# Chunk attention: dividing by the row sums after the values' product in place of before it

## The chip, the cores and the metric

The kernel runs on one core of one Trainium2 chip. The metric is the device time of one execution in microseconds (us); the median of three runs of the kernel before is 1773.39 us (1770.58 to 1775.37).

## What is computed

The program is a two-layer encoder for 512 tokens of width 1024, all in 32-bit floats. The second layer begins with chunked softmax attention: 16 heads of 64 columns, chunks of 64 tokens that see themselves and all earlier ones here, with a learned bias by distance. Cut to what matters:

```python
s = jnp.einsum('bqhd,bkhd->bhqk', q_c, k_c) * scale + bias
s = jnp.where((band_pos + start) >= 0, s, -1e30)
p = jax.nn.softmax(s, axis=-1)
return jnp.einsum('bhqk,bkhd->bqhd', p, v_c)
# all chunks: o, then o @ w_out
```

## The kernel before

The engines are programmed by hand: each has its own instruction list in a fixed order, and they meet only at semaphores. TensorE (PE) multiplies, VectorE (DVE) and ScalarE (ACT) work on its results in PSUM (8 banks of 128x512), GpSimd (POOL) masks the bias, and SyncE issues DMAs.

Chunk attention works through 8 pairs of heads, m = 0 to 7; e = 0, 1 is the head in the pair, i = 0 to 3 a block of 128 queries, which needs keys 0 to (i+1)*128, so blocks have 128 to 512 columns. For a pair:

- `ca_scores_pe` multiplies queries with keys in the order i = 3, 2, 0, 1, both heads side by side on 64 rows of the array each; the last, i = 1, waits for the first two sums of the same pair, which free its bank. `sums` on VectorE adds the bias, takes the maximum of each row (`c_s2`, L2039) and negates it (`c_max`, L2043).
- `exp` on ScalarE (L2011) makes the unnormalized probabilities and their row sums; `rescale` on VectorE (L2053, L2057) takes the reciprocals and multiplies the probabilities in place.
- `ca_turn_p_pe` transposes them (L1959) in eight groups n = 0 to 7 (s = n // 2 is the block of keys, e = n % 2), through a ring of three PSUM banks, 4 to 6. `ca_copy` takes each group to SBUF: n = 0, 2, 5, 7 on ScalarE (L1985), n = 1, 3, 4, 6 on VectorE (L1987), by the list `COPY`. A group can be written once the copy three groups earlier is done.
- `ca_values_pe` (L1969) multiplies values with these, both heads side by side on 64 columns of the array each, into bank 7. ScalarE rounds the result to `c_oT[0]` (out_hi here, L2028), and VectorE keeps the rest in `c_oT[1]` (`out_lo`, L2047). The output projection "co" multiplies with both and waits for the last `out_lo`.

The pairs are staggered by the order in each list. In round m TensorE does turns(m), scores(m+2), values(m). ScalarE waits for the maxima of m+1 and then does the eight exps of m+1 with its four copies of m between them, and at the end of the round waits for values(m) and does out_hi(m). VectorE does out_lo(m-1), its copies of m with the rescale of (m+1, e=0) before the last, sums(m+2), and the rescale of (m+1, e=1).

Of the kernel before, what the change touches and what calls it, by code (L numbers as in the profile page):

```python
# [7 lines left out]
F32 = mybir.dt.float32  # L8
F32R = mybir.dt.float32r
ALU = mybir.AluOpType  # L10
ACT = mybir.ActivationFunctionType
AX = mybir.AxisListType.X

P = 128
D = 1024
SEQ = 512
# [3 lines left out]
TT = SEQ // P  # L20
# [17 lines left out]
CH = 16  # L38
CD = D // CH
# [8 lines left out]
LEVELS = 5  # L48
# [27 lines left out]
def build_program(nc, A):  # L76
    ctx = ExitStack()
    with ctx:
        def tensor_at(name, at, dtype, *shape):

            assert at % 8 == 0
            with nc.sbuf_tensor(f"below_{name}", [P, at], F32), nc.sbuf_tensor(name, [P, *shape], dtype) as v:
                return v[(slice(None),) * (1 + len(shape))]

        def rounded(name, at, *shape):
            return tensor_at(name, at, F32R, *shape)

        with nc.sbuf_tensor("params", [P, N_PAR], F32) as par:
# [4 lines left out]
        ps = ctx.enter_context(nc.psum_tensor("ps", [P, 8, 512], F32))  # L93
# [15 lines left out]
                   "glu_landed": ("wab_in", 16), "g_v": ("u_s", 8),  # L109
                   "cat_hi": ("go_sq", TT), "cat_lo": ("go_n", TT), "mem_kept": ("cat_s5", 1),  # L110
                   "f_gate": ("sv_y", LEVELS * TT), "f_rmm": ("r_kw", 2 * NCH), "f_rbc": ("r_om", NCH), "eps_rows": ("sv_d", LEVELS * TT),
                   "c_pv2": ("sv_u", LEVELS * TT),
                   "c_mask": ("sv_mask", LEVELS * TT), "c_rec": ("sv_yc", LEVELS * TT),
                   "s5_gate": ("s5_fn", 4), "g_roots": ("s5_den", 1), "g_coef": ("s5_arg", 1), "logit_rows": ("s5_dt", 1), "logit_turned": ("s5_rd", 1),
                   "s5_pad": ("conv", 12), "y_v": ("conv", 20), "y_a": ("u_s", 4)}
# [24 lines left out]
        def sem(name):  # L140
            name = named(name)[0]
            if name not in sems:
                sems[name] = ctx.enter_context(nc.semaphore(name))
            return sems[name]
# [55 lines left out]
        ident = ccol("ident")  # L200
# [142 lines left out]
        def after(name, n):  # L343

            return n + named(name)[1]
# [1082 lines left out]
        at_b, at_c, at_d, at_e, at_f = (arena + 4096 * n for n in range(1, 6))  # L1428
# [416 lines left out]
        c_max, c_neg, c_sum, c_rec = cs(2, 2, TT), cs(2, 2, TT), cs(2, 2, TT), cs(2, 2, TT)  # L1845
        ck_rows = rows(high_b)
        cqT, ckT = feat(high_c), feat(high_d)
        CA_ROWS, CA_EXP = (3, 2, 0, 1), (3, 2, 1, 0)
        CA_TRI = P * TT * (TT + 1) // 2

        def p_c(m, e, i):
            at = base + (2 * (m % 2) + e) * CA_TRI + P * (i * (i + 1) // 2)
            return reg(at, (i + 1) * P)

        def pT_c(e, s):
            at = base + (4 + e) * CA_TRI + P * (s * TT - s * (s - 1) // 2)
            return reg(at, (TT - s) * P)
# [3 lines left out]
            return ps[:, bank + e, c0:c0 + (i + 1) * P]  # L1861

        c_oT = (rounded("c_o_hi", arena, KT, SEQ), rounded("c_o_lo", at_b, KT, SEQ))


        def ca_proj_pe(pe):
# [83 lines left out]
        def ca_turn_p_pe(pe, m):  # L1950
            for n in range(8):
                s, e = n // 2, n % 2
                g = 8 * m + n
                if g >= 3:
                    pe.wait_ge(sem(COPY[(g - 3) % 8][0]), 4 * ((g - 3) // 8) + COPY[(g - 3) % 8][1])
                for i in range(s, TT):
                    if s == 0:
                        pe.wait_ge(sem(RESCALE[i][0]), after(RESCALE[i][0], RESCALE[i][1] * (2 * m + e) + RESCALE[i][2]))
                    ins = pe.transpose(ps[:, 4 + g % 3, i * P:(i + 1) * P], p_c(m, e, i)[:, s * P:(s + 1) * P], ident)  # L1959
                ins.then_inc(sem("c_tr"), 1)  # L1960

        def ca_values_pe(pe, m):
            if m > 0:
                pe.wait_ge(sem("c_ol"), m)
            for s in range(TT):
                for e in range(2):
                    pe.wait_ge(sem(COPY[2 * s + e][0]), 4 * m + COPY[2 * s + e][1])
                    h = 2 * m + e
                    ins = pe.matmul(ps[64 * e:64 * e + 64, 7, s * P:SEQ], v_rows[:, s, h * CD:(h + 1) * CD], pT_c(e, s),  # L1969
                                    start=(s == 0), stop=(s == TT - 1), skip_group_check=True)  # L1970
            ins.then_inc(sem("c_o"), 1)


        COPY = [("c_pa", 1), ("c_pv", 1), ("c_pa", 2), ("c_pv", 2), ("c_pv", 3), ("c_pa", 3), ("c_pv", 4), ("c_pa", 4)]
        RESCALE = [("c_pv2", 4, 4), ("c_pv2", 4, 3), ("c_pv2", 4, 2), ("c_pv2", 4, 1)]

        def ca_copy(eng, m, n):
            s, e = n // 2, n % 2
            g = 8 * m + n
            eng.wait_ge(sem("c_tr"), g + 1)  # L1980
            if m >= 1:
                eng.wait_ge(sem("c_o"), m)
            dst, src = pT_c(e, s), ps[:, 4 + g % 3, s * P:SEQ]
            if COPY[n][0] == "c_pa":
                eng.activation(dst, src, ACT.Copy).then_inc(sem("c_pa"), 1)  # L1985
            else:
                eng.tensor_copy(dst, src).then_inc(sem("c_pv"), 1)  # L1987
# [20 lines left out]
        def ca_act(a):  # L2008
            def exp(m, e, i):
                p = p_c(m, e, i)  # L2010
                a.activation(p, p, ACT.Exp, bias=c_neg[:, m % 2, e, i:i + 1], accum_out=c_sum[:, m % 2, e, i:i + 1]).then_inc(sem("c_exp"), 1)  # L2011

            a.wait_ge(sem("c_max"), 1)
            for e in range(2):
                for i in CA_EXP:
                    exp(0, e, i)
            for m in range(CH // 2):
                if m + 1 < CH // 2:
                    a.wait_ge(sem("c_max"), m + 2)
                for e in range(2):  # L2020
                    for j in range(4):
                        if m + 1 < CH // 2:
                            exp(m + 1, e, CA_EXP[j])
                        n = 4 * e + j
                        if COPY[n][0] == "c_pa":
                            ca_copy(a, m, n)
                a.wait_ge(sem("c_o"), m + 1)
                a.activation(c_oT[0][:, m, :].rearrange("p (i n) -> p i n", i=TT),  # L2028
                                  ps[:, 7, :].rearrange("p (i n) -> p i n", i=TT)[:, :, ::-1], ACT.Copy).then_inc(sem("c_oc"), 1)

        def ca_dve(v):
            def sums(m):
                v.wait_ge(sem("c_mask"), after("c_mask", 2 * m + 2))
                if m >= 2:
                    v.wait_ge(sem("c_tr"), 8 * (m - 1))
                for n, i in enumerate(CA_ROWS):
                    v.wait_ge(sem("c_s"), 4 * m + (1, 3, 3, 4)[n])
                    for e in range(2):
                        v.tensor_tensor_reduce(out=p_c(m, e, i), in0=ca_score(i, e),  # L2039
                                                    in1=bias_ring[:, (2 * m + e) % 4, BAND_W - (i + 1) * P:BAND_W], scale=1.0, scalar=-3.0e38,  # L2040
                                                    op0=ALU.add, op1=ALU.max, accum_out=c_max[:, m % 2, e, i:i + 1]).then_inc(sem("c_s2"), 1)
                v.wait_ge(sem("c_s2"), 8 * m + 8)
                v.tensor_scalar(c_neg[:, m % 2], c_max[:, m % 2], -1.0, None, ALU.mult).then_inc(sem("c_max"), 1)  # L2043

            def out_lo(m):
                v.wait_ge(sem("c_oc"), m + 1)
                v.tensor_tensor(c_oT[1][:, m, :].rearrange("p (i n) -> p i n", i=TT),  # L2047
                                ps[:, 7, :].rearrange("p (i n) -> p i n", i=TT)[:, :, ::-1],
                                c_oT[0][:, m, :].bitcast(F32).rearrange("p (i n) -> p i n", i=TT), ALU.subtract).then_inc(sem("c_ol"), 1)

            def rescale(m, e):
                v.wait_ge(sem("c_exp"), 8 * m + 4 * e + 4)
                v.reciprocal(c_rec[:, m % 2, e], c_sum[:, m % 2, e]).then_inc(sem("c_rec"), 1)  # L2053
                v.wait_ge(sem("c_rec"), after("c_rec", 2 * m + e + 1))
                for i in (3, 2, 1, 0):
                    p = p_c(m, e, i)
                    v.tensor_scalar(p, p, c_rec[:, m % 2, e, i:i + 1], None, ALU.mult).then_inc(sem("c_pv2"), 1)  # L2057

            sums(0)
            sums(1)  # L2060
            rescale(0, 0)
            rescale(0, 1)
            for m in range(CH // 2):
                if m > 0:
                    out_lo(m - 1)
                for n in range(8):
                    if COPY[n][0] == "c_pv":
                        ca_copy(v, m, n)
                    if n == 4 and m + 1 < CH // 2:
                        rescale(m + 1, 0)  # L2070
                if m + 2 < CH // 2:
                    sums(m + 2)
                if m + 1 < CH // 2:
                    rescale(m + 1, 1)
            out_lo(CH // 2 - 1)

        def ca_pool(g):
# [371 lines left out]
```

## Time and profile before

| | before |
|---|---|
| median of three runs | 1773.39 us |
| the profiled execution, own time | 1774.5 us |
| its span on the core | 1772.7 us |
| mean granted TensorE clock | 0.982 |
| busy in the span: TensorE, VectorE, ScalarE | 94%, 44%, 34% |
| chunk attention's rounds | about 1084 to 1171 us of the span |

One execution was traced. A row of one line of the code has the least, median and longest duration in ns and the first and last start in us. A row of the timeline is: start in us from the span's start, duration in us, engine, line, operation, output and input, shape, count; in brackets the idle time of the engine before it and what ended it. PEclk is the clock that TensorE was granted as a share of 2.4 GHz. A 32-bit product is two records of TensorE, a transpose is one. An engine may start its next instruction some 0.1 us before the one before has ended, so what an instruction occupies is read from start to start.

### The profile page before, as it was taken

Reading aid. Unit: us, or ns where it says so; the run is one execution under the profiler, and the core shown is the slowest. Engines: PE = TensorE matmul, PEld = TensorE weight load, DVE = VectorE, ACT = ScalarE, POOL = GpSimd, SP = SyncE. Lnnn points to the kernel's source line nnn. Section 1 sums busy time; section 2 is a strip of 40 time slices with the busy share of each in tenths; the row PEclk is TensorE's granted clock in tenths of the full one; section 3 lists DMA queues with packets and bytes.
Section 4 is the critical chain, followed back from the end, with each engine's and each line's share of the span. In section 5 each row is a group of like instructions: output and inputs, shape, how many; then the busy total and the mean of one; then the engine's idle time right before and its main releaser. Section 6 shows DMA issues by size and latency. Waiting matters only on the chain.

```text
span 1772.7 us, 22589 instructions
## 1 busy us (share of the span) xinstructions
PE 1659.4 (94%) x9358; PEld 1354.6 (76%) x9358; DVE 786.1 (44%) x1023; ACT 611.5 (34%) x991; POOL 230.0 (13%) x305
## 2 busy tenths in 40 slices
PE   6998589999989999999999998899998999999999
PEld 5887568777858888888888885468776878888887
DVE  5752834545353444443225436844444444444222
ACT  5224143345342432222114335634353332332110
POOL 2681223310000111111000000000000011111000
PEclk9996899999999999999999998999999999999999
DMA  6306001125202233332222330304410333333221
GB/s 206 96 24 119 1 5 58 63 95 189 72 24 69 74 97 101 101 104 95 95 95 88 102 119 24 96 24 137 147 50 24 96 95 95 95 95 95 95 95 71
DMA packets 146801, 151.85 MB, mean 86 GB/s; under 512 B 8864, under 2 KB 109344, under 8 KB 146592
## 3 DMA queue, kind: packets, MB, share of 16 engines
q1 hardware_dynamic: 146720, 150.69, 27.8%
q8 instruction: 60, 0.98, 0.2%
q14 instruction: 21, 0.17, 0.0%
HBM read 147.53 MB, written 3.15 MB: 85 GB/s over the span
## 4 chain that ended last, share of the span: by engine, by line
PE 86%; DVE 8%; ACT 3%; issue 2%; DMA 0%; SPq 0%; POOL 0%; DVEq 0%; ACTq 0%
PE ps L325 24%; PE ps L327 24%; PE ps L326 23%; PE ps L1612 2%; PE ps L1635 2%; PE ps L1969 1%; PE ps L955 1%; DVE sb L2039 1%; PE ps L1070 1%; ACT w_hi L293 1%; PE ps L1229 1%; PE ps L417 1%; ACT sb L2011 1%; PE ps L1240 1%; DVE sb L2057 1%
## 5 line engine op out<-in xcount | busy, mean ns | idle before, releaser
L325 PE MATMUL ps<-h_hi,w_hi 128*128 128x512 f32 x864 | 336.9, 390 | 4.0 <-DVE w_lo L1783 3.9
L326 PE MATMUL ps<-h_lo,w_hi 128*128 128x512 f32 x864 | 336.1, 389 | 0.0
L297 DVE TENSOR_TENSOR w_lo<-raw,w_hi 128x2048 fp32r<-128x2048 f32 x70 | 160.4, 2292 | 395.4 <-ACT w_hi L293 395.4
L293 ACT ACTIVATE w_hi<-raw 128x2048 fp32r<-128x2048 f32 x84 | 160.7, 1915 | 421.2 <-PE ps L327 420.6
L327 PE MATMUL ps<-h_hi,w_lo 128*128 128x512 f32 x704 | 273.9, 389 | 0.0
L325 PEld LDWEIGHTS ps<-h_hi,w_hi 128*128 128x128 f32 x864 | 162.2, 188 | 38.5 <-issue 4.7
L326 PEld LDWEIGHTS ps<-h_lo,w_hi 128*128 128x128 f32 x864 | 162.2, 188 | 33.7
L1783 DVE TENSOR_TENSOR w_lo<-raw,w_hi 128x2048 fp32r<-128x2048 f32 x44 | 138.1, 3138 | 53.5 <-ACT w_hi L1765 53.5
L327 PEld LDWEIGHTS ps<-h_hi,w_lo 128*128 128x128 f32 x704 | 132.1, 188 | 27.5
L1765 ACT ACTIVATE w_hi<-raw 128x2048 fp32r<-128x2048 f32 x44 | 84.3, 1916 | 160.9 <-PE ps L327 160.9
L325 PE MATMUL ps<-w_hi,a_hi 128*128 128x512 f32 x352 | 137.3, 390 | 1.7 <-DVE up L1781 1.7
L326 PE MATMUL ps<-w_lo,a_hi 128*128 128x512 f32 x352 | 137.0, 389 | 0.0
L327 PE MATMUL ps<-w_hi,a_lo 128*128 128x512 f32 x352 | 136.9, 389 | 0.0
L1793 POOL CAST a_hi<-up 128x512 f32 x44 | 27.0, 613 | 843.0 <-DVE up L1781 843.0
L325 PE MATMUL ps<-w_hi,h_hi 128*128 128x512 f32 x320 | 124.7, 390 | 2.3 <-DVE h_lo L430 2.3
L327 PE MATMUL ps<-w_hi,h_lo 128*128 128x512 f32 x320 | 124.5, 389 | 0.0
L326 PE MATMUL ps<-w_lo,h_hi 128*128 128x512 f32 x320 | 124.5, 389 | 0.0
L1781 DVE TENSOR_TENSOR up<-up,ps 128x512 f32<-128x512 f32 x44 | 30.3, 688 | 192.4 <-PE ps L327 188.6
L1761 ACT ACTIVATE up<-up 128x512 f32<-128x512 f32 x44 | 27.8, 632 | 152.0 <-DVE up L1777 152.0
L325 PEld LDWEIGHTS ps<-w_hi,a_hi 128*128 128x128 f32 x352 | 66.1, 188 | 16.0 <-DVE up L1781 2.5
L327 PEld LDWEIGHTS ps<-w_hi,a_lo 128*128 128x128 f32 x352 | 66.1, 188 | 13.9
L326 PEld LDWEIGHTS ps<-w_lo,a_hi 128*128 128x128 f32 x352 | 66.1, 188 | 13.7
(369 smaller groups left out, 2686.1 us busy)
## 6 DMA issues: line engine op xcount, KB each, us to landing
raw<-in_f_w_gate SPq DMA_DIRECT2D x44, 512.0 KB, 4.0
raw<-in_f_w_up SPq DMA_DIRECT2D x44, 512.0 KB, 5.2
raw<-in_f_w_down SPq DMA_DIRECT2D x44, 512.0 KB, 4.1
raw<-in_xa_w_kv SPq DMA_DIRECT2D x16, 1024.0 KB, 5.0
raw<-in_c_w_qkv SPq DMA_DIRECT2D x12, 1024.0 KB, 5.0
raw<-in_ab_w_in SPq DMA_DIRECT2D x10, 1024.0 KB, 5.3
raw<-in_xa_w_q SPq DMA_DIRECT2D x8, 1024.0 KB, 5.1
raw<-in_xa_w_out SPq DMA_DIRECT2D x8, 1024.0 KB, 5.0
```

The costliest lines, as they stand in the source:

```text
L293: a.activation(w_hi[:, n % 2, :], raw[n % 2], ACT.Copy).then_inc(sem("w_hi"), 1)
L297: v.tensor_tensor(w_lo(n)[:, n % 2, :], raw[n % 2], w_hi[:, n % 2, :].bitcast(F32), ALU.subtract).then_inc(sem("w_lo"), 1)
L325: pe.matmul(out, a[0], b[0], start=start, stop=False)
L326: pe.matmul(out, a[0], b[1], start=False, stop=False)
L327: return pe.matmul(out, a[1], b[0], start=False, stop=stop)
L1612: ins = pe.matmul(ps[:, 2 * (h % 2) + i // 2, (i % 2) * 256:(i % 2) * 256 + 256], qT[:, 2 * h + d, i * P:(i + 1) * P], xk_T[:, 2 * h + d, ...
L1635: ins = pe.matmul(ps[:, 6 + d, :], xv[:, s, h * XD + d * P:h * XD + (d + 1) * P], pT_x[h % 2][:, s, :], start=(s == 0), stop=(s == 1))
L1761: a.activation(gsil[:, s, :], gsil[:, s, :], ACT.Silu).then_inc(sem(f"f{l}_silu"), 1)
L1765: a.activation(w_hi[:, slot, :], raw[slot], ACT.Copy).then_inc(sem("w_hi"), 1)
L1781: v.tensor_tensor(prod[:, s, :], gsil[:, s, :], ps[:, 2 * s + 1, :], ALU.mult).then_inc(sem(f"f{l}_free"), 1)
L1783: v.tensor_tensor(w_lo(n0)[:, slot, :], raw[slot], w_hi[:, slot, :].bitcast(F32), ALU.subtract).then_inc(sem("w_lo"), 1)
L1793: g.tensor_copy(aT[0][:, at], prod[:, s, :]).then_inc(sem(f"f{l}_ahi"), 1)
```

## The change

The probabilities are no longer multiplied. `rescale` is gone; one reciprocal of a 128x8 block for each pair (`reciprocals`) takes its place. After its eight groups of transposes TensorE has a ninth: eight products of a 128x64 broadcast of the reciprocals with the identity, both heads side by side on 64 columns of the array each, into bank 6, once the copy of group 5 is done. They spread the reciprocals over a block laid out as the output is. ScalarE copies that block to SBUF (`c_rbc`, two buffers) at the end of its round. VectorE multiplies the values' output in bank 7 with it into the same buffer (`out_scaled`), ScalarE rounds from there (`out_hi`), now in the next round between its second and third exp, and VectorE's `out_lo` follows after copy 3. The transposes wait for the exps alone, and values(m) waits for `out_scaled(m-1)` where it waited for `out_lo(m-1)`. The ring of three banks is counted anew in each round (n % 3), with the ninth group in it.

```diff
         def ca_turn_p_pe(pe, m):
             for n in range(8):
                 s, e = n // 2, n % 2
-                g = 8 * m + n
-                if g >= 3:
-                    pe.wait_ge(sem(COPY[(g - 3) % 8][0]), 4 * ((g - 3) // 8) + COPY[(g - 3) % 8][1])
+                bank_copied(pe, m, n)
                 for i in range(s, TT):
                     if s == 0:
-                        pe.wait_ge(sem(RESCALE[i][0]), after(RESCALE[i][0], RESCALE[i][1] * (2 * m + e) + RESCALE[i][2]))
-                    ins = pe.transpose(ps[:, 4 + g % 3, i * P:(i + 1) * P], p_c(m, e, i)[:, s * P:(s + 1) * P], ident)
+                        pe.wait_ge(sem("c_exp"), 8 * m + 4 * e + CA_EXP.index(i) + 1)
+                    ins = pe.transpose(ps[:, 4 + n % 3, i * P:(i + 1) * P], p_c(m, e, i)[:, s * P:(s + 1) * P], ident)
                 ins.then_inc(sem("c_tr"), 1)
+            bank_copied(pe, m, 8)
+            pe.wait_ge(sem("c_rec"), after("c_rec", m + 1))
+            for i in range(TT):
+                for e in range(2):
+                    ins = pe.matmul(ps[64 * e:64 * e + 64, 6, i * P:(i + 1) * P], c_rec[:, m % 2, e, i:i + 1].broadcast_to([P, CD]), ident,
+                                    start=True, stop=True)
+            ins.then_inc(sem("c_tr"), 1)
 
         def ca_values_pe(pe, m):
             if m > 0:
-                pe.wait_ge(sem("c_ol"), m)
+                pe.wait_ge(sem("c_om"), after("c_om", m))
...
+        def bank_copied(pe, m, n):
+            m, n = (m, n - 3) if n >= 3 else (m - 1, n + 6)
+            if m >= 0 and n < 8:
+                pe.wait_ge(sem(COPY[n][0]), 4 * m + COPY[n][1])
+            elif m >= 0:
+                pe.wait_ge(sem("c_rb"), after("c_rb", m + 1))
...
+            def out_hi(m):
+                a.wait_ge(sem("c_om"), after("c_om", m + 1))
+                a.activation(c_oT[0][:, m, :], c_rbc(m), ACT.Copy).then_inc(sem("c_oc"), 1)
...
-                a.wait_ge(sem("c_o"), m + 1)
-                a.activation(c_oT[0][:, m, :].rearrange("p (i n) -> p i n", i=TT),
-                                  ps[:, 7, :].rearrange("p (i n) -> p i n", i=TT)[:, :, ::-1], ACT.Copy).then_inc(sem("c_oc"), 1)
+                        if n == 1 and m > 0:
+                            out_hi(m - 1)
+                a.wait_ge(sem("c_tr"), 9 * m + 9)
+                if m >= 2:
+                    a.wait_ge(sem("c_ol"), m - 1)
+                a.activation(tiles(c_rbc(m)), tiles(ps[:, 6, :])[:, :, ::-1], ACT.Copy).then_inc(sem("c_rb"), 1)
+            out_hi(CH // 2 - 1)
...
+            def out_scaled(m):
+                v.wait_ge(sem("c_o"), m + 1)
+                v.wait_ge(sem("c_rb"), after("c_rb", m + 1))
+                v.tensor_tensor(tiles(c_rbc(m)), tiles(ps[:, 7, :])[:, :, ::-1], tiles(c_rbc(m)), ALU.mult).then_inc(sem("c_om"), 1)
...
-            def rescale(m, e):
-                v.wait_ge(sem("c_exp"), 8 * m + 4 * e + 4)
-                v.reciprocal(c_rec[:, m % 2, e], c_sum[:, m % 2, e]).then_inc(sem("c_rec"), 1)
-                v.wait_ge(sem("c_rec"), after("c_rec", 2 * m + e + 1))
-                for i in (3, 2, 1, 0):
-                    p = p_c(m, e, i)
-                    v.tensor_scalar(p, p, c_rec[:, m % 2, e, i:i + 1], None, ALU.mult).then_inc(sem("c_pv2"), 1)
+            def reciprocals(m):
+                v.wait_ge(sem("c_exp"), 8 * m + 8)
+                v.reciprocal(c_rec[:, m % 2], c_sum[:, m % 2]).then_inc(sem("c_rec"), 1)
...
             sums(0)
             sums(1)
-            rescale(0, 0)
-            rescale(0, 1)
+            reciprocals(0)
             for m in range(CH // 2):
                 if m > 0:
-                    out_lo(m - 1)
+                    out_scaled(m - 1)
                 for n in range(8):
                     if COPY[n][0] == "c_pv":
                         ca_copy(v, m, n)
-                    if n == 4 and m + 1 < CH // 2:
-                        rescale(m + 1, 0)
+                    if n == 3 and m > 0:
+                        out_lo(m - 1)
                 if m + 2 < CH // 2:
                     sums(m + 2)
                 if m + 1 < CH // 2:
-                    rescale(m + 1, 1)
+                    reciprocals(m + 1)
+            out_scaled(CH // 2 - 1)
             out_lo(CH // 2 - 1)
```

## Rows read from the trace of the kernel before

**Rows 1.** The page: the chain that ended last, by engine.
```profile
PE 86%; DVE 8%; ACT 3%; issue 2%; DMA 0%; SPq 0%; POOL 0%; DVEq 0%; ACTq 0%
```
**Rows 2.** Windows: length; busy (count) of PE, PEld, DVE, ACT, POOL; PEclk; DMA.
```profile
1123.89:1133.57 9.68, 7.90 (x56) 4.55 (x54) 8.74 (x34) 6.24 (x22) 0.29 (x2) 1.00 0.21 56
```
**Rows 3.** Timeline, one round, from scores(4) to the next sums.
```profile
1122.51 2.00 PE L1947 MATMUL ps<-sb 64*128 64x512 f32 x12
...
1123.89 0.69 DVE L2039 CUSTOM_DVE_ANT_0 sb<-ps,sb 128x512 f32<-128x512 f32 x1
...
1125.25 0.70 PE L1947 MATMUL ps<-sb 64*128 64x256 f32 x4 [0.74 <-DVE sb L2039]
...
1125.88 2.37 PE L1969 MATMUL ps<-sb 128*64 128x512 f32 x16
...
1127.30 0.17 DVE L2043 TENSOR_SCALAR sb<-sb 128x8 f32<-128x8 f32 x1
...
1128.19 0.66 PE L1959 MATMUL ps<-sb 128*128 128x128 f32 x4
1128.30 0.60 ACT L2028 ACTIVATE c_o_hi<-ps 128x512 fp32r<-128x512 f32 x1 [3.44 <-PE ps L1969]
1128.80 0.71 ACT L2011 ACTIVATE sb<-sb 128x512 f32<-128x512 f32 x1
...
1133.57 0.69 DVE L2039 CUSTOM_DVE_ANT_0 sb<-ps,sb 128x512 f32<-128x512 f32 x1
```
**Rows 4.** Timeline, one round: a rescale, ScalarE's copies 0 and 5.
```profile
1119.83 0.58 ACT L1985 ACTIVATE sb<-ps 128x512 f32<-128x512 f32 x1
...
1122.50 1.28 DVE L2057 TENSOR_SCALAR sb<-sb 128x512 f32<-128x512 f32 x4
...
1123.45 0.37 ACT L1985 ACTIVATE sb<-ps 128x256 f32<-128x256 f32 x1
```
**Rows 5.** By form, 1084:1176, VectorE: xcount | busy, mean ns | idle before.
```profile
L1987 DVE COPY sb<-ps 128x512 f32<-128x512 f32 x8 | 5.5, 691 | 1.7 <-PE ps L1959 1.4
...
L2047 DVE TENSOR_TENSOR c_o_lo<-ps,c_o_hi 128x512 fp32r<-128x512 f32 x8 | 5.5, 690 | 3.5 <-ACT c_o_hi L2028 3.1
...
L2053 DVE RECIPROCAL sb<-sb 128x4 f32<-128x4 f32 x16 | 2.8, 175 | 2.8 <-ACT sb L2011 2.8
```
**Rows 6.** Timeline, ScalarE from SBUF to SBUF, 128x512, and the next.
```profile
598.12 0.63 ACT L1761 ACTIVATE up<-up 128x512 f32<-128x512 f32 x1
598.66 1.90 ACT L1765 ACTIVATE w_hi<-raw 128x2048 fp32r<-128x2048 f32 x1
```
**Rows 7.** TensorE, timeline and line: broadcast by identity; pairs on 64 columns.
```profile
595.12 1.05 PE L1743 MATMUL ps<-sb 128*128 128x128 f32 x8
595.93 0.48 PE L325 MATMUL ps<-h_hi,w_hi 128*128 128x512 f32 x1
...
L844 PE MATMUL ps<-sb x128: 222/222/271, 174.4 to 178.1; 128*64 128x64 f32 x128
```
**Rows 8.** Timeline: scores(1), sums(1), first exp of pair 1, sums(2), sums(7).
```profile
1090.65 4.62 PE L1947 MATMUL ps<-sb 64*128 64x512 f32 x16 [0.88 <-DVE sb L2039]
...
1092.88 0.69 DVE L2039 CUSTOM_DVE_ANT_0 sb<-ps,sb 128x512 f32<-128x512 f32 x1 [2.08 <-PE ps L1947]
...
1096.88 0.72 ACT L2011 ACTIVATE sb<-sb 128x512 f32<-128x512 f32 x1 [1.58 <-DVE sb L2043]
...
1104.53 0.69 DVE L2039 CUSTOM_DVE_ANT_0 sb<-ps,sb 128x512 f32<-128x512 f32 x1
...
1152.91 0.68 DVE L2039 CUSTOM_DVE_ANT_0 sb<-ps,sb 128x512 f32<-128x512 f32 x1
```
**Rows 9.** Timeline, the end of the stage.
```profile
1171.49 0.50 PE L325 MATMUL ps<-w_hi,c_o_hi 128*128 128x512 f32 x1 [1.42 <-DVE c_o_lo L2047]
```
**Rows 10.** Timeline and window (as rows 2): the stage's start, after a wait.
```profile
1088.54 1.22 PE L1947 MATMUL ps<-sb 64*128 64x256 f32 x4 [2.76 <-DVE sb L2039]
...
1089.00:1091.00 2.00, 1.12 (x6) 0.40 (x6) 1.76 (x11) 0.17 (x1) 0.00 (x0) 0.50 0.00 0
```

More of the change, by code:

```diff
@@ L111, in build_program @@
                    "f_gate": ("sv_y", LEVELS * TT), "f_rmm": ("r_kw", 2 * NCH), "f_rbc": ("r_om", NCH), "eps_rows": ("sv_d", LEVELS * TT),
-                   "c_pv2": ("sv_u", LEVELS * TT),
+                   "c_rb": ("sv_u", LEVELS * TT), "c_om": ("sv_t", (LEVELS - 1) * TT),
                    "c_mask": ("sv_mask", LEVELS * TT), "c_rec": ("sv_yc", LEVELS * TT),
@@ L1863, in build_program, with c_rbc, tiles @@
         c_oT = (rounded("c_o_hi", arena, KT, SEQ), rounded("c_o_lo", at_b, KT, SEQ))
+        c_rbc2 = tensor_at("c_rbc", at_f + 2056, F32, 2, SEQ)
+        def c_rbc(m):
+            return c_rbc2[:, m % 2, :]
+        def tiles(o):
+            return o.rearrange("p (i n) -> p i n", i=TT)
         def ca_proj_pe(pe):
@@ L1974, in build_program @@
         COPY = [("c_pa", 1), ("c_pv", 1), ("c_pa", 2), ("c_pv", 2), ("c_pv", 3), ("c_pa", 3), ("c_pv", 4), ("c_pa", 4)]
-        RESCALE = [("c_pv2", 4, 4), ("c_pv2", 4, 3), ("c_pv2", 4, 2), ("c_pv2", 4, 1)]
+        def bank_copied(pe, m, n):
[4 more added lines that the diff above has]
+                pe.wait_ge(sem("c_rb"), after("c_rb", m + 1))
         def ca_copy(eng, m, n):
             s, e = n // 2, n % 2
-            g = 8 * m + n
-            eng.wait_ge(sem("c_tr"), g + 1)
+            eng.wait_ge(sem("c_tr"), 9 * m + n + 1)
             if m >= 1:
                 eng.wait_ge(sem("c_o"), m)
-            dst, src = pT_c(e, s), ps[:, 4 + g % 3, s * P:SEQ]
+            dst, src = pT_c(e, s), ps[:, 4 + n % 3, s * P:SEQ]
             if COPY[n][0] == "c_pa":
@@ L2034, in sums @@
                 if m >= 2:
-                    v.wait_ge(sem("c_tr"), 8 * (m - 1))
+                    v.wait_ge(sem("c_tr"), 9 * (m - 1))
                 for n, i in enumerate(CA_ROWS):
@@ L2043, in sums @@
                 v.tensor_scalar(c_neg[:, m % 2], c_max[:, m % 2], -1.0, None, ALU.mult).then_inc(sem("c_max"), 1)
+            def out_scaled(m):
+                v.wait_ge(sem("c_o"), m + 1)
+                v.wait_ge(sem("c_rb"), after("c_rb", m + 1))
+                v.tensor_tensor(tiles(c_rbc(m)), tiles(ps[:, 7, :])[:, :, ::-1], tiles(c_rbc(m)), ALU.mult).then_inc(sem("c_om"), 1)
             def out_lo(m):
                 v.wait_ge(sem("c_oc"), m + 1)
-                v.tensor_tensor(c_oT[1][:, m, :].rearrange("p (i n) -> p i n", i=TT),
-                                ps[:, 7, :].rearrange("p (i n) -> p i n", i=TT)[:, :, ::-1],
-                                c_oT[0][:, m, :].bitcast(F32).rearrange("p (i n) -> p i n", i=TT), ALU.subtract).then_inc(sem("c_ol"), 1)
-            def rescale(m, e):
-                v.wait_ge(sem("c_exp"), 8 * m + 4 * e + 4)
-                v.reciprocal(c_rec[:, m % 2, e], c_sum[:, m % 2, e]).then_inc(sem("c_rec"), 1)
-                v.wait_ge(sem("c_rec"), after("c_rec", 2 * m + e + 1))
-                for i in (3, 2, 1, 0):
-                    p = p_c(m, e, i)
-                    v.tensor_scalar(p, p, c_rec[:, m % 2, e, i:i + 1], None, ALU.mult).then_inc(sem("c_pv2"), 1)
+                v.tensor_tensor(c_oT[1][:, m, :], c_rbc(m), c_oT[0][:, m, :].bitcast(F32), ALU.subtract).then_inc(sem("c_ol"), 1)
+            def reciprocals(m):
+                v.wait_ge(sem("c_exp"), 8 * m + 8)
+                v.reciprocal(c_rec[:, m % 2], c_sum[:, m % 2]).then_inc(sem("c_rec"), 1)
             sums(0)
             sums(1)
-            rescale(0, 0)
-            rescale(0, 1)
+            reciprocals(0)
             for m in range(CH // 2):
                 if m > 0:
-                    out_lo(m - 1)
+                    out_scaled(m - 1)
                 for n in range(8):
```

## The prediction, made before the changed kernel was run

> **What bounds the kernel now.** I read the page's chain first: TensorE carries 86% of what ended last [rows 1]. Over the whole kernel, then, work taken from VectorE is worth nothing; it can only count where TensorE waits for it. The window of one attention round shows such a place: of 9.68 us VectorE is busy 8.74, TensorE 7.90, ScalarE 6.24 [rows 2]. So the first impression is that VectorE sets the round here, and the change takes work from it. But busy time alone doesn't say what the round will be afterwards; for that one has to follow the order of the lists. The timeline of one round gives this order and its delays [rows 3]. I call T the start of a round's sums (1123.89 us). From there: the second sum lets TensorE do the last scores at T+1.36, values follow at T+1.99, the maxima are negated at T+3.41 and known at T+3.58, and the next round's transposes start at T+4.30 and end at T+4.96. The next sums start at T+9.68. ScalarE waits 3.44 us for values(m) before its out_hi, so it has room.
>
> **What VectorE loses and gains.** Per pair it loses two rescales, 2 x 1.28 us [rows 4], and one of two reciprocals of 0.18 [rows 5]. It gains out_scaled, which the trace doesn't have; the nearest row is out_lo, a product of the same shape from PSUM, 0.69 [rows 5]. In all about 2.0 us less in each round. That would be a gain if VectorE's list ran without new gaps. It won't.
>
> **The new order on ScalarE and TensorE.** The ninth group goes into bank 6 and waits for the copy of group 5. That is ScalarE's third copy, and its list puts six of the next pair's exps, two other copies and now out_hi(m-1) ahead of it. TensorE's list is in order: scores(m+2) stand behind the ninth group, and VectorE's next sums wait for scores(m+2). Before, the last transposes waited only for VectorE's copies, and scores started at 1122.51, while copy 5 started only at 1123.45 [rows 3, 4]. So a loop closes: sums, maxima, ScalarE's exps and copies, ninth group, scores, sums. I walk it with T as above:
> - The exp of (m+2, e=0, i=3) can start at T+3.6 and is done before the transposes are; so copy 0 starts when group 0 has been transposed, T+4.96+0.03 = T+4.99.
> - From copy 0 to copy 5 ScalarE's list took 1123.45 - 1119.83 = 3.62 us without a gap [rows 4]. Out_hi now stands in it. Its operation is not in the trace; another activation of 128x512 from SBUF to SBUF takes 0.63 and lets the next start after 598.66 - 598.12 = 0.54 [rows 6]. Copy 5 takes 0.37 [rows 4]. It ends at T + 4.99 + 3.62 + 0.54 + 0.37 = T+9.52, and TensorE starts the ninth group at T+9.57.
> - The ninth group has no row. Four products of a 128x128 broadcast with the identity occupy TensorE for 595.93 - 595.12 = 0.81 us [rows 7]; here there are eight of half the width. If the two heads run side by side the time is that, about 0.85; if not, double, 1.7. Pairs on 64 columns elsewhere: 128 records of 64 columns in 3.7 us; 16 records of 128 columns are a quarter of that work, 0.94 [rows 7]. I take 0.95, as this row is the nearest, and keep 0.8 and 1.7 as the ends.
> - Scores start at T+10.52. Their first pair of products took 2.23 from start to the first sum at half clock, 1090.65 to 1092.88 [rows 8]; at full clock 1.12 and a hop of 0.04. The next sums start at T+11.68.
>
> The round becomes 11.68 us where it was 9.68: 2.0 us longer. VectorE lies beside it with slack: its out_scaled, three of its copies and out_lo are done some 2 us before copy 5, and it then idles until the new sums. So the 2.0 us saved on VectorE turn into waiting, ScalarE's copy of the reciprocals' block (0.60, like the old out_hi from PSUM [rows 3]) runs while TensorE does scores and costs nothing, and the round is longer by what TensorE now waits for ScalarE.
>
> **The first round and the end.** In round 0 no rescale delays the transposes and there is no out_hi. ScalarE starts pair 1's exps at 1096.88 [rows 8]; copy 5 starts 0.71 [rows 3] + 3.62 = 4.33 us later, at 1101.2, and ends at 1101.6. Ninth group and scores, 0.05+0.95+1.16, put sums(2) at 1103.75, where they were at 1104.53 [rows 8]: 0.8 us gained at full clock. At half clock the last two terms double, and 1.3 are lost; I take the gain, since the wait before it gets shorter. From sums(2) to sums(7) are 5 rounds, 1104.53 to 1152.91 [rows 8]: 5 x 2.0 = 10.0 us lost.
> From sums(7) to the first product of "co" were 1171.49 - 1152.91 = 18.58 us [rows 8, 9]. Now, with T at sums(7): the ninth group of pair 6 at T+9.57, no scores, values(6) from T+10.52 to T+12.75 (2.23 to occupy; from 1125.88 to the next group at 1128.19 it is 2.31 with a hop [rows 3]). Pair 7 has no rescale and no exps beside it, but its copies pass through the ring: VectorE starts out_scaled(6) when values(6) end, T+13.0, and is done with it at T+13.7; copy 1 ends at T+14.6 (0.69 [rows 5], behind its group's transposes), copy 3 at T+15.2, out_lo(6) at T+15.8, copy 4 at T+16.2 (the narrower copies at less in proportion); group 7 waits for it, the ninth group runs T+16.35 to T+17.30, values(7) until T+19.68. Then, one after the other, out_scaled 0.69, out_hi 0.63 and out_lo 0.69 with hops of 0.05, 2.2 in all. Co starts at T+21.9: 3.3 us lost.
> Sum: -0.8 + 10.0 + 3.3 = 12.5 us. The profiled execution took 1774.5 us, so 1787.0; against the median of 1773.4 the same sum gives 1786. The output projection's weights come ahead of their use in either case, and everything behind simply shifts.
>
> **A rule beside a row.** The last pair of scores occupies TensorE for 1125.88 - 1125.25 = 0.63 us until values start [rows 3], though 256 columns at the values' rate (1280 columns in 2.31 us) would be 0.46: a change of the array's shape seems to cost up to 0.17. The Trainium skill (TensorEngine Tiling (Array Packing), Key Properties) says that changing the tiling mode drains the TensorE. The ninth group stands between full-width transposes and scores on 64 rows, so it adds one such change. By the rule I would add 0.17 for each of its places on the loop, seven: 1787; without it 1786, which I keep.
>
> **The rivals.**
> - *It pays, VectorE was the bound.* If copy 5 did not hold TensorE, the round would be what TensorE itself needs: its 7.90 us [rows 2] with the ninth group less overlap, 8.0 to 8.85. Then 5 rounds gain 0.8 to 1.7 each, the first gains up to 2.9 (two rescales and reciprocals, [rows 4, 5]) and the end loses 0.8: 1763 to 1770. It decides for this if the ninth group starts before T+7.5, 2 us earlier than the loop gives it; ScalarE would have to run four of its exps less ahead of copy 5. Nothing in the rows speaks for it. 8 in 100.
> - *It evens out.* Some step on the loop is shorter and the round stays near 9.7: 1769 to 1778. 5 in 100.
> - *The loop, with the heads of the ninth group one after the other.* 0.75 us more in seven places, 5 in all: 1791. The row of pairs on 64 columns speaks against it. 8 in 100.
> - *The granted clock falls.* TensorE now waits about 1.5 us in a stretch for copy 5, besides 0.7 for the sums. After a wait of 2.76 us at the start of the stage the clock read 0.50, that is 1.2 GHz [rows 10]; with waits up to 0.74 it reads 1.00 [rows 2, 3]. In between there is no row. At half clock the parts of TensorE on the loop (scores and values 2.9, group 0 0.4, the ninth group 0.95, first scores 1.1) double, 5.4 us a round; if that holds for half of the rounds, 13 more: 1799, for all, 1813. 9 in 100.
> - *The loop as worked out,* 1781 to 1791: 70 in 100.
>
> **How the numbers follow.** The likeliest gives 1786. The lower end takes a ninth group of 0.8, an out_hi that costs less, a start that gains more and the spread of the runs (1770.6 to 1775.4): 1780. The upper end takes the ninth group at 1.7 or a few rounds at the lower clock: 1796. A measurement tells some 0.3% from no change, 5.3 us: slower is the loop in its three forms, 0.87; same 0.05; faster 0.08.
>
> **What would show it.** In the trace of the changed kernel: rounds of about 11.7 us between first sums; TensorE idle 1.2 to 1.8 us before the ninth group, released by ScalarE's copy; the ninth group 0.85 to 1.1 us; VectorE idle about 3 us before the sums, released by the scores; co starting near 1184. The prediction is wrong if the ninth group doesn't wait for ScalarE, or if the round is under 10.5 us.

## The result, and the profile after

The changed kernel takes 1797.4 us (median of 4 runs) against 1772.0: 1.0142 times the time of before, with a 95% interval of 1.0125 to 1.0159. It is slower, as forecast, but by 25 us where 12.5 were forecast, and 1797.4 lies just outside the range of 1780 to 1796. The profiled execution took 1797.5 us in all, its span 1795.8; it is 23.0 us longer than the profiled execution of the kernel before.

First the timeline of one round of the changed kernel, in the same columns as [rows 3]:

```profile
1117.02 0.69 DVE L2065 CUSTOM_DVE_ANT_0 sb<-ps,sb 128x512 f32<-128x512 f32 x1 [4.51 <-PE ps L1955]
...
1118.39 0.30 PEld L1955 LDWEIGHTS ps<-sb 64*128 64x128 f32 x4 [0.33 <-DVE sb L2065]
...
1121.33 2.32 PE L1965 MATMUL ps<-sb 128*128 128x128 f32 x16
...
1122.02 0.60 ACT L2003 ACTIVATE sb<-ps 128x512 f32<-128x512 f32 x1 [0.52 <-PE ps L1965]
...
1123.12 0.62 ACT L2033 ACTIVATE c_o_hi<-c_rbc 128x512 fp32r<-128x512 f32 x1
...
1124.65 0.65 PE L1965 MATMUL ps<-sb 128*128 128x128 f32 x4 [1.01 <-ACT sb L2003]
...
1126.18 0.37 ACT L2003 ACTIVATE sb<-ps 128x256 f32<-128x256 f32 x1
...
1126.61 1.09 PE L1971 MATMUL ps<-sb 128*64 128x128 f32 x16 [1.30 <-ACT sb L2003]
...
1127.63 2.00 PE L1955 MATMUL ps<-sb 64*128 64x512 f32 x12
...
1128.94 0.69 DVE L2065 CUSTOM_DVE_ANT_0 sb<-ps,sb 128x512 f32<-128x512 f32 x1 [3.42 <-PE ps L1955]
```

The loop of the prediction is there, place by place. With T = 1117.02: copy 0 at T+5.00 (worked out: 4.99), copy 5 at T+9.16 (9.15), the ninth group (L1971) at T+9.59 (9.57), released by ScalarE's copy after TensorE had waited 1.30 us. VectorE waits 3.42 us for the scores (L1955). This round took 11.92 us. The next one starts alike and then goes another way. The same lines, from the ninth group on:

```profile
1138.11 0.36 ACT L2003 ACTIVATE sb<-ps 128x256 f32<-128x256 f32 x1
...
1138.52 1.98 PE L1971 MATMUL ps<-sb 128*64 128x128 f32 x16 [1.29 <-ACT sb L2003]
...
1140.43 2.60 PE L1955 MATMUL ps<-sb 64*128 64x512 f32 x12
...
1142.36 0.69 DVE L2065 CUSTOM_DVE_ANT_0 sb<-ps,sb 128x512 f32<-128x512 f32 x1 [4.91 <-PE ps L1955]
```

ScalarE's copy 5 and the ninth group start where they should, T+9.17 and T+9.58 with T = 1128.94, but the ninth group occupies TensorE for 1.91 us and not 1.02, and the round becomes 13.42. The windows of these microseconds (length, TensorE busy, PEclk, DMA) say why:

```profile
1135.12:1136.57 1.45, 0.44 (x3) 1.00 0.21 81
1137.23:1138.52 1.29, 0.00 (x0) 0.91 0.00 0
1138.52:1139.50 0.98, 0.98 (x10) 0.50 0.00 0
1139.50:1140.40 0.90, 0.90 (x10) 0.50 0.00 0
1140.40:1141.40 1.00, 1.00 (x4) 0.50 0.00 0
1141.40:1142.40 1.00, 1.00 (x8) 0.85 0.00 0
1142.40:1143.70 1.30, 0.63 (x8) 1.00 0.00 0
```

The granted clock is 1.00 while TensorE waits for copy 2 and falls during its wait for copy 5, to 0.50, 1.2 GHz; there it stays through the ninth group and half of the scores. In the other long rounds it falls at the start of the ninth group or inside it, at about 1114.4, 1152.0 and 1165.6 us. By round, from first sum to first sum:

```profile
1104.01:1117.02 13.01, 10.25 (x70) 0.89 0.14 41
1117.02:1128.94 11.92, 9.47 (x72) 0.97 0.18 46
1128.94:1142.36 13.42, 10.43 (x72) 0.87 0.13 39
1142.36:1155.89 13.53, 10.54 (x72) 0.87 0.62 195
```

The fifth takes 13.55. The 0.97 of the round of 11.92 is the rest of the low stretch before it: the clock reads 0.50 in its first 0.8 us and 1.00 from there on. [Rows 2] had 9.68 us at 1.00. The start of the stage has waits and a low clock as in [rows 10]. The clock is back at 1.00 from 1094 us and falls again in the first ninth group, at about 1100.7:

```profile
1100.26 1.55 PE L1971 MATMUL ps<-sb 128*64 128x128 f32 x16 [1.30 <-ACT sb L2003]
1101.74 3.17 PE L1955 MATMUL ps<-sb 64*128 64x512 f32 x12
```

Sums(2) and sums(7) begin at 1104.01 and 1169.44 us, where [rows 8] had 1104.53 and 1152.91. At the end of the stage, in place of [rows 9]:

```profile
1179.02 1.80 PE L1971 MATMUL ps<-sb 128*64 128x128 f32 x16 [1.30 <-ACT sb L2003]
1180.61 3.35 PE L1982 MATMUL ps<-sb 128*64 128x512 f32 x16
1183.89 2.87 PE L1965 MATMUL ps<-sb 128*128 128x128 f32 x19
...
1187.62 1.09 PE L1971 MATMUL ps<-sb 128*64 128x128 f32 x16
1188.55 2.32 PE L1982 MATMUL ps<-sb 128*64 128x512 f32 x16
1193.05 0.79 PE L325 MATMUL ps<-w_hi,c_o_hi 128*128 128x512 f32 x1 [2.18 <-DVE c_o_lo L2078]
```

The ninth group and the values of pair 6 run at the lower clock here too (values 3.28 us from start to start where 2.31 are usual [rows 3]), and so do the first products of co.

### The profile page after: what moved, and what is told of

Read it like the earlier page. It is cut to its first block, busy times and chain, and to the rows that moved or that the text cites. A ratio compares the mean times of both kernels' runs of the same rounds, so it can differ in the third digit from the quotient of the medians.

```text
span 1795.8 us, 22811 instructions
## 1 busy us (share of the span) xinstructions
PE 1676.7 (93%) x9486; PEld 1366.5 (76%) x9486; DVE 770.6 (43%) x959; ACT 616.9 (34%) x999; POOL 230.0 (13%) x305
## 4 chain that ended last, share of the span: by engine, by line
PE 86%; DVE 8%; ACT 4%; issue 2%; DMA 0%; SPq 0%; POOL 0%; DVEq 0%; ACTq 0%
PE ps L325 23%; PE ps L327 23%; PE ps L326 23%; PE ps L1612 2%; PE ps L1635 2%; PE ps L1982 1%; PE ps L1955 1%; ACT sb L2029 1%; PE ps L955 1%; DVE sb L2065 1%; PE ps L1971 1%; ACT w_hi L293 1%; PE ps L1229 1%; PE ps L417 1%; PE ps L1240 1%
```

## The experiments

Each time is told by its ratio to the kernel before on the same chip, with its 95% interval. For the stage itself I give three times from the trace: from the first sum of pair 0 to that of pair 2, the five rounds from there to pair 7, and from there to co's first product. The code ahead of the stage is the same in all, yet the first sum falls anywhere between 1082.9 and 1090.8 us of the span, so the stage is measured from its own start.

| kernel | to pair 2 | five rounds | end | stage against before | ratio |
|---|---|---|---|---|---|
| before | 17.35 | 48.38 | 18.58 | | |
| changed | 18.21 | 65.43 | 23.61 | +22.9 | 1.0142 |
| e1_warm | 16.79 | 59.60 | 22.78 | +14.9 | 1.0068 |
| e2_gap | 14.41 | 48.98 | 23.61 | +2.7 | 0.9993 |
| e3_hi_late | 18.29 | 61.23 | 21.40 | +16.6 | 1.0092 |
| e4_copy5 | 17.14 | 54.60 | 20.99 | +8.4 | 1.0039 |
| e5_ninth1 | 17.19 | 59.17 | 22.90 | +15.0 | 1.0078 |
| e6_no_rescale | 14.40 | 48.09 | 18.24 | -3.6 | 0.9980 |
| e7_gap_order | 14.41 | 46.38 | 20.15 | -3.4 | 0.9986 |
| e8_gap_order2 | 13.90 | 44.88 | 19.51 | -6.0 | 0.9967 |

A ratio of 0.001 is 1.8 us. Between the stage's difference and that of the whole lie up to 4 us (e2), which no run explains. Both ends of the span scatter: the time ahead of the stage by up to 8 us, as said, and the time from co's first product to the end of the span between 599.6 and 602.8 us.

### e1_warm: more work for TensorE in its two waits

```diff
+        def keep_busy(pe, m):
+            pe.wait_ge(sem("c_s2"), 8 * min(m + 2, CH // 2))
+            pe.matmul(ps[:, 0, :], ident, con[:, 0:SEQ], start=True, stop=True)
...
+                if n == 5:
+                    keep_busy(pe, m)
                 bank_copied(pe, m, n)
...
+            keep_busy(pe, m)
             bank_copied(pe, m, 8)
```

> The changed kernel plus 16 products of 512 columns whose result nobody reads (0.85 us each at full clock), two a round, placed where TensorE waits for ScalarE's copies 2 and 5. Theory of loop and clock: the round is set by the loop sums, exps, copy 5, ninth group, scores, and on top of it the waits let the granted clock fall, which costs 1.1 to 1.6 us in four of five rounds and more at the end. Then TensorE kept busy stays at clock 1.00, every round is 11.9 us (after: 13.0, 11.9, 13.4, 13.5, 13.6), the first product of co starts near 1186 us instead of 1193, and the time is 6 to 9 us below the changed kernel: 1.009 to 1.011 of before, although there is more work. Rival, TensorE's added work is what costs (0.9 us of ninth group a round) and the clock is only a companion: 13.6 us more work gives 1.015 to 1.022.

Measured 1.0068 (1.0051 to 1.0085), below the expected 1.009. All five rounds take 11.92 us. The timeline of a round, with the added products at L1960:

```profile
1129.93 1.02 PE L1960 MATMUL ps<-sb 128*128 128x512 f32 x2
...
1131.11 0.66 PE L1971 MATMUL ps<-sb 128*128 128x128 f32 x4
...
1131.60 1.02 PE L1960 MATMUL ps<-sb 128*128 128x512 f32 x2
...
1133.06 1.09 PE L1978 MATMUL ps<-sb 128*64 128x128 f32 x16 [0.44 <-ACT sb L2010]
```

and its window (length; busy of PE, PEld, DVE, ACT, POOL; PEclk; DMA):

```profile
1123.48:1135.39 11.91, 10.64 (x76) 5.93 (x74) 6.86 (x24) 6.98 (x22) 0.29 (x2) 1.00 0.14 44
```

The idle time before the ninth group shrinks from 1.30 us to 0.44, the one before the transposes that wait for copy 2 from 1.01 to almost nothing; the rest of the round stays in its place and the clock reads 1.00. TensorE has 16 more products to do, of 1.02 us each in the timeline, and the kernel is about 13 us faster than the changed one (1.0142 - 1.0068). The traces hold 11.0 of these: 8.1 in the stage, and 3.0 because the first sum came that much earlier, which the added products can't have caused. So the time that a round took over 11.92 came from the granted clock, and the rival in which TensorE's load costs has fallen. The run filled both waits and doesn't tell them apart.

At the end of the stage the added products stand in the way themselves. In the last pair the transposes start at 1171.99 us and the ninth group at 1176.59, 4.60 us later, where the changed kernel needed 3.73 (1183.89 to 1187.62):

```profile
1171.99 2.31 PE L1971 MATMUL ps<-sb 128*128 128x128 f32 x16
1176.59 1.09 PE L1978 MATMUL ps<-sb 128*64 128x128 f32 x16
```

That is 0.9 us which e1 pays and the changed kernel doesn't.

### e2_gap: the ninth group where TensorE waits anyway

```diff
+        def ca_ninth_pe(pe, m):   # the lines of the ninth group, moved here
...
                 if n == 3:
+                    if m >= 2:
+                        ca_ninth_pe(pe, m - 2)
                     pe.wait_ge(sem("c_s2"), 8 * m + 2)
...
-                    v.wait_ge(sem("c_tr"), 9 * (m - 1))
+                    v.wait_ge(sem("c_tr"), 9 * (m - 1) - 1)
```

> The ninth group of round m moves from behind the transposes into scores(m+2), ahead of their last pair of products, where TensorE waits 0.7 us for two sums anyway; for the last two pairs it stays. All other work is the same. Theory of the loop: copy 5 no longer stands between the transposes and the sums, the round falls to 9.3 to 9.8 us, the clock stays at 1.00, co starts at 1170 to 1174 us, and the time is that of the kernel before, 0.998 to 1.002. Rival, the work of the ninth group and out_scaled costs wherever it is put: rounds stay at 10.5 us or more, 1.005 or above.

The sums now wait for the eight groups of transposes only, since the ninth stands behind them. Measured 0.9993 (0.9983 to 1.0002): no difference from the kernel before, and 26 us less than the changed kernel with the same work. Rounds take 9.79 or 9.80 us at clock 1.00. Timeline:

```profile
1118.24 1.09 PE L1949 MATMUL ps<-sb 128*64 128x128 f32 x16
...
1119.27 0.70 PE L1966 MATMUL ps<-sb 64*128 64x256 f32 x4
...
1125.53 0.66 PE L1976 MATMUL ps<-sb 128*128 128x128 f32 x4 [1.01 <-ACT sb L2009]
...
1126.11 2.00 PE L1966 MATMUL ps<-sb 64*128 64x512 f32 x12
...
1127.42 0.69 DVE L2071 CUSTOM_DVE_ANT_0 sb<-ps,sb 128x512 f32<-128x512 f32 x1 [1.02 <-PE ps L1966]
```

The ninth group (L1949) takes its 1.03 us beside the sums, of which TensorE would have waited 0.7, and the scores follow the transposes without a wait for copy 5. What is left is the wait of 1.01 us for copy 2. The end is as long as in the changed kernel, since the last two pairs keep the old order. What cost the 2 us a round was the place of the ninth group in TensorE's list. In the stage e2 is 2.7 us longer than the kernel before: 5.0 at the end and 0.6 in the five rounds, less 2.9 ahead of pair 2.

### e3_hi_late: out_hi behind copy 7

```diff
-                        if n == 1 and m > 0:
-                            out_hi(m - 1)
+                if m > 0:
+                    out_hi(m - 1)
                 a.wait_ge(sem("c_tr"), 9 * m + 9)
...
-                    if n == 3 and m > 0:
-                        out_lo(m - 1)
+                    if n == 3 and m > 1:
+                        out_lo(m - 2)
```

> The changed kernel with out_hi(m-1) at the end of ScalarE's round m, behind copy 7, in place of between its second and third exp; out_lo goes one round later. Same work. Theory of the loop: copy 5 ends 0.52 us earlier, a round at full clock takes 11.4 us and not 11.9, 3 us less over the stage before any effect on the clock: 1.009 to 1.013. Rival, ScalarE's order doesn't set the round: 1.014 as before and rounds of 11.9.

Measured 1.0092 (1.0076 to 1.0109). Rounds of 11.39, 13.02, 12.65, 11.39 and 12.78 us: those without a fallen clock are 0.53 below 11.92, which is what out_hi occupied on the loop. Where the clock falls is now another set of rounds.

### e4_copy5: copy 5 to VectorE, copy 6 to ScalarE

```diff
-        COPY = [("c_pa", 1), ("c_pv", 1), ("c_pa", 2), ("c_pv", 2), ("c_pv", 3), ("c_pa", 3), ("c_pv", 4), ("c_pa", 4)]
+        COPY = [("c_pa", 1), ("c_pv", 1), ("c_pa", 2), ("c_pv", 2), ("c_pv", 3), ("c_pv", 4), ("c_pa", 3), ("c_pa", 4)]
```

> The changed kernel with copy 5 on VectorE and copy 6 on ScalarE. Theory of the loop: the ninth group no longer waits for ScalarE's two exps of the second head, only for copy 2 and VectorE; it starts about 1.0 us earlier, rounds of 10.9 us at full clock and one long wait of TensorE in a round instead of two, so the clock falls less: 1.004 to 1.010. Rival, the round is set by TensorE's work: unchanged, 1.014.

Measured 1.0039 (1.0025 to 1.0053). All five rounds take 10.92 us, 1.00 us less than at full clock before. Windows of two of them:

```profile
1101.57:1112.49 10.92, 8.93 (x72) 1.00 0.16 49
1112.49:1123.41 10.92, 8.93 (x72) 1.00 0.17 50
```

The wait for copy 2 is still 1.0 us in each round, and the clock stays at 1.00: with this one wait, the 0.7 us for the sums and 0.3 us ahead of the ninth group it doesn't fall in these rounds, with 1.3 us in place of the 0.3 it does.

### e5_ninth1: two of the ninth group's eight products

```diff
-            for i in range(TT):
+            for i in range(1):
                 for e in range(2):
                     ins = pe.matmul(ps[64 * e:64 * e + 64, 6, i * P:(i + 1) * P], ...
```

> The changed kernel with two of the ninth group's eight products, those of the first block of queries; for the other blocks the outputs are divided by what bank 6 held. All waits stay. Theory of the loop: what the products occupy, 1.02 us at full clock, shrinks to about 0.25, so a round at full clock takes 11.15 us where it took 11.92; the waits for copies 2 and 5 stay and the clock still falls in some rounds: 1.008 to 1.011. Rival, the wait for copy 5 alone is what costs: rounds of 11.9, 1.013 or more.

Measured 1.0078 (1.0060 to 1.0097), a little below what was expected. Rounds of 11.26, 12.08, 11.28, 11.56 and 12.99 us: the two shortest have the lower clock only in their first 0.9 and 1.4 us, beside the sums, and are 0.66 below 11.92, 0.1 less of a saving than worked out. The six products are worth 0.66 us a round. The rest of the 2.1 us that e2 took off a round lies in the wait ahead of the ninth group and in its other two products.

### e6_no_rescale: the kernel before without the rescale

```diff
-                        pe.wait_ge(sem(RESCALE[i][0]), after(RESCALE[i][0], RESCALE[i][1] * (2 * m + e) + RESCALE[i][2]))
+                        pe.wait_ge(sem("c_exp"), 8 * m + 4 * e + CA_EXP.index(i) + 1)
...
-                for i in (3, 2, 1, 0):
-                    p = p_c(m, e, i)
-                    v.tensor_scalar(p, p, c_rec[:, m % 2, e, i:i + 1], None, ALU.mult).then_inc(sem("c_pv2"), 1)
```

> The kernel before with rescale's 64 products on VectorE left out and nothing in their place, so the probabilities stay unnormalized: the most that taking work from VectorE can bring in this order. Theory of the loop: ScalarE's chain lies right behind VectorE's. Out_hi, exp and copy 0 start at T+4.4, +4.9 and +5.6, copy 2 ends at T+7.7, transposes end and scores start at about T+8.3, so the next sums come at T+9.4 where they came at 9.68; only the first and the last round gain more, some 3 us together, and 1.3 over the rest: 0.996 to 0.999 of before. Rival, VectorE's busy time set the round: 2.0 us or more off each round, 15 us in all, 0.991.

Measured 0.9980 (0.9970 to 0.9989). The rounds fall from 9.68 to 9.62 us, by 0.06 and not by 0.3; of the 3.6 us that the stage gains, 3.0 are ahead of pair 2. A part of these 3.0 may be the clock: in the kernel before it read 0.50 from 1098.6 to 1100 us, at the first transposes, after a wait of 3.02 us for the rescale, and e6 has the same transposes at 1.00. Waits from 1104 to 1150 us, five rounds (who waited for whom: us, times, longest):

```profile
ACT c_o_hi L2028 <- PE ps L1969: 16.9, 5, 3.4
...
PEld ps L1959 <- ACT sb L1985: 8.5, 10, 0.9
DVE c_o_lo L2047 <- ACT c_o_hi L2028: 7.3, 5, 1.5
```

With 2.56 us a round less to do, VectorE waits up to 1.5 us for out_hi. The chain through ScalarE (values, out_hi, exp, copy 0) was right behind VectorE's all along. So even for nothing, the removal was worth 3.5 us of 1773.

### e7 and e8: a better order for the changed work

e7_gap_order is e2_gap with the list of copies of e4_copy5, out_hi after the exp behind copy 2 (`n == 3` in place of `n == 1`) and out_lo behind copy 6 (`n == 6`).

> The kernel of the second run (ninth group inside the scores) with copy 5 on VectorE and copy 6 on ScalarE, out_hi one exp later, behind copy 2, and out_lo behind VectorE's last copy. Theory of the loop: copy 2 is now the link, and out_hi leaves its way, so the round falls from 9.79 to 9.0 to 9.3 us: 0.995 to 0.999. Rival, TensorE's work and order set the 9.79 now: unchanged, 0.999 to 1.000.

Measured 0.9986 (0.9976 to 0.9996), rounds of 9.27 to 9.28 us. e8_gap_order2 goes further, with out_lo behind copy 5:

```diff
+        COPY = [("c_pa", 1), ("c_pv", 1), ("c_pv", 2), ("c_pa", 2), ("c_pv", 3), ("c_pv", 4), ("c_pa", 3), ("c_pa", 4)]
+        ACT_AFTER = {(0, 0): 0, (0, 1): 3, (0, 3): 6, (1, 1): 7}
...
+                        if (e, j) in ACT_AFTER:
+                            ca_copy(a, m, ACT_AFTER[e, j])
+                        if (e, j) == (0, 2) and m > 0:
+                            out_hi(m - 1)
...
             for s in range(TT):
+                if s == 2 and m + 2 >= CH // 2:
+                    ca_ninth_pe(pe, m)
```

> The same with copy 2 on VectorE and copies 3, 6 and 7 early on ScalarE, out_hi behind the third exp, and in the last two rounds the ninth group inside values, between their second and third block, where values wait for copy 5 anyway. Theory of the loop: no transpose waits for a copy behind two exps, rounds of 8.5 to 9.0 us, and an end of 20 to 22 us from the last first sum to co where the changed kernel had 23.6: 0.993 to 0.997. Rival as before: rounds of 9.8, 0.999 to 1.000.

Measured 0.9967 (0.9953 to 0.9980), rounds of 8.97 us, an end of 19.5. TensorE from the transposes to the scores, and VectorE's first sum:

```profile
1122.33 3.16 PE L1976 MATMUL ps<-sb 128*128 128x128 f32 x20
...
1125.41 1.13 PE L1966 MATMUL ps<-sb 64*128 64x512 f32 x4
```

All twenty transposes of the pair now run as one stretch of 3.1 us, where the changed kernel had 5.3 us from the first of them to the ninth group. This version beats the kernel before by 6 us and the changed one by 31. How much of the 6 us belongs to the new order alone isn't shown: no run gives the kernel before, or e6, a better order of copies and out_hi.

## Why the prediction was wrong

- *What bounds the round.* Right: VectorE's busy time didn't say what its relief would bring. e6 measures it: 0.06 us a round.
- *The new loop.* Right in mechanism and in place; e2, e3, e4 and e5 each cut one term out of it, and the rounds at full clock moved by 2.1, 0.53, 1.00 and 0.66 us.
- *Its length.* 11.68 worked out, 11.92 measured. Out_hi occupied 0.52 (0.54 forecast). The ninth group took 1.02 where I took 0.95. The scores took 1.31 to the first sum where I took 1.16 from half of a row at half clock [rows 8]. The chain of the changed kernel shows that step:

```profile
1127.70 1.08 PE ps L1955 x4
1128.78 0.03 issue
1128.81 0.05 DVEq L2063
1128.86 0.08 issue
1128.94 1.32 DVE sb L2065 x4
```

  TensorE's own part is 1.08 us, and 0.16 more pass until VectorE starts, with its sequencer (DVEq) among them. From the start of the scores to the first sum, 1.31 - 1.08 = 0.23 us go beside TensorE's part; in the row that I halved it was 2.23 - 2 x 1.08 = 0.07. That row was of scores(1) and sums(1). These sums don't wait for transposes as those of later rounds do, and these scores don't follow products of another shape. Which of the two makes the difference wasn't tried. In e2, where the ninth group isn't ahead of the scores but full-width transposes are, the same step takes 1.31 too. With 0.04 of small differences ahead of the ninth group, 0.24 us a round: 1.2 us in five.
- *The step that failed* is the choice of full clock for the sum, "at full clock 1.12", and with it "The granted clock falls" as a rival of 9 in 100. I had a row at 0.50 after a wait of 2.76 us and rows at 1.00 with waits up to 0.74, and counted the range between as unlikely. The prediction says "In between there is no row", but [rows 9] was one: after the wait of 1.42 us ahead of co the clock stayed at 1.00 in the kernel before:

```profile
1171.49:1180.00 8.51, 8.51 (x37) 1.00 0.01 2
```

  A single wait of this length spoke for full clock. In the loop, with waits of 1.0 and 1.3 us in the same round, the clock fell in four rounds of five. e1 shows what that was worth. Held at 1.00, the five rounds take 59.6 us and not 65.4: the clock cost 5.8 there, 1.2 a round. It cost 1.4 more before pair 2. At the end e1 is only 0.8 shorter, but 0.9 of its own are the added products: 1.7. In all the clock cost 8.9 us of the stage, and the mis-sized loop 1.4 (0.24 in six places). With the 12.5 of the sum that makes 22.8; the stage grew by 22.9. So the sum was right for full clock. That the whole of e1 costs 12 us (1.0068) is near 12.5 by luck: its stage is 14.9 longer, the same 12.5 with 1.4 and 0.9 on top. The rival was priced at 5.4 us for each round at the lower clock and 13 for half of them; that its 1799 lies near the measured 1797.4 is luck too, since low stretches covered little more than the ninth group and a part of the scores. Behind the stage, from co's first product to the end of the span, the changed kernel took 602.8 us and the kernel before 601.2. Co's first products run there at the lower clock, but e6, at 1.00 there, took 602.7, so these 1.6 us are no price of the clock that a run shows.
- *The first round.* A gain of 0.8 forecast; from the first sum of pair 0 it is 0.9 us longer. The first ninth group starts where it was worked out, 8.76 us after the first sum of pair 1 (8.77). It and the scores behind it then took 3.75 us where 2.11 were in the sum, since the clock, at 1.00 during the waits, fell again inside the ninth group. The prediction had a price for that, 1.3 lost, and didn't take it.
- *The end.* 3.3 us forecast, 5.0 measured. Ninth group and values of pair 6 took 1.59 and 3.28 us at the lower clock where 0.95 and 2.23 were in the sum, which is the whole difference. In e1, at 1.00, they took 0.92 and 2.25.
- *The direction and the other rivals.* Slower was right. The heads of the ninth group run side by side (1.02 us, not 1.7). The condition for a gain, a ninth group that needn't wait for copy 5, is the one that e2, e7 and e8 build, and e7 and e8 gain, with their copies and out_hi in another order as well.
- *The rule on changes of the array's shape.* The Trainium skill (TensorEngine Tiling (Array Packing), Key Properties) lets TensorE drain at each. The trace agrees in sign: at full clock the ninth group occupied 1.02 us ahead of scores, which have another shape, and 0.93 ahead of values, which have its own (1187.62 to 1188.55). That is 0.1 us and not the 0.17 of the prediction. The other 0.15 of the difference of 0.24 lies behind the scores' start and was no part of the rule's estimate.

## What to carry to other kernels

Work taken from the busiest engine of a loop is worth what the next chain behind it leaves free; leave the work out for one run to see that price before building what replaces it. Work that is added belongs where its engine waits anyway: the same eight products cost 26 us behind the transposes, some 9 of them by the lower clock, and nothing inside the scores. And a wait of TensorE has two prices, its own length and the slower clock of what follows, so a sum that puts new waits of about 1 us into each round has to be made at both clocks.

## What was not expected of the hardware

- Two waits of 1.0 and 1.3 us in a round of 11.9 let the granted clock fall to 0.50 in four rounds of five; one wait of 1.0 in a round of 10.9 (e4), or waits filled with useless products until 0.44 of the longer one was left (e1), did not. Why the clock held in the waits of the one round stays open, and so does whether each wait alone would do. A single wait of 1.42 us ahead of co left it at 1.00 in the kernel before.
- At the lower clock the ninth group took 1.91 us from start to start, 1.02 at the full one: 1.87 times.
